# Roots and reciprocals of the norms, taken token by token on a few columns in a two-block transformer kernel

## The chip, the cores and the metric

The kernel runs on one core of a Trainium2 chip. The metric is device time in microseconds (us), the median of several executions. The engines are TensorE (PE; PEld is its weight load), VectorE (DVE), ScalarE (ACT), GpSimd (POOL) and SyncE (SP), which issues most DMAs.

## The reference

Everything is float32. The input is one sequence of 256 tokens of width 1024, with 256 context and 256 memory tokens. The first block has two layers (latent attention, a Fourier mix and a convolution side by side, then an MLP); the second has one (RWKV-7, S5 and gated linear attention side by side, then cross attention, then a gated MLP). Between them stand the norms that this change is about. Each takes one number per token, or per token and head:

```python
def rms_norm(x, g):
    xf = x.astype(jnp.float32)
    y = xf * lax.rsqrt(jnp.mean(jnp.square(xf), axis=-1, keepdims=True) + EPS)
    return (y * g.astype(jnp.float32)).astype(x.dtype)
...
# in rwkv7_mix
kk = kk * lax.rsqrt(jnp.sum(kk * kk, axis=-1, keepdims=True) + 1e-12)
y = ((y - mean) * lax.rsqrt(var + RWKV_GN_EPS)).reshape(B, L, MIX_W) * ln_w + ln_b
# in gla_mix
o = o * lax.rsqrt(jnp.mean(o * o, axis=-1, keepdims=True) + 1e-5) * norm_g
```

## The kernel before

Activations lie with features on the 128 partitions and tokens on the free axis: `xT` and `hT` are 128 x 8 x 512 (8 feature tiles; 256 context tokens, then 256 tokens of x). Layer 0 of the first block works on all 512 tokens (`s` is 0:512), layer 1 and the second block on the last 256 (`xs`), except where keys of the context are needed.

**Order.** Each engine has its own instruction stream, written out by hand and in order. `did` (a helper) raises a semaphore behind an instruction, and mostly waits for it too. PSUM has 8 banks: `open_bank(key, pool)` in PE's stream takes the next one of a pool in turn and waits until its last user has freed it; `finished(engine, key)` waits until PE has filled it, `taken(engine, key)` until its reader has freed it. The pool "run" has banks 0 to 4 (and 7 in the second block), the pool "hold" has 5 and 6. The weights, most of the 247 MB read from HBM, come through `ring`, four slots of 1 MB, loaded by SP in the order of their use; PE frees a slot as it goes on to the next. A float32 matmul shows as two MATMUL and two LDWEIGHTS records in the trace, a transpose as one.

**A norm.** ACT squares the features into `sq` (L1257); for most norms POOL adds the first six or seven tiles (L1655). PE multiplies the squares by a 128x128 matrix of ones (`norm_stat_step`, `stat`), so that every partition of the bank holds the sum of each token. ACT takes the root of the bank, 128 x 256 or 128 x 512 elements, into `rinv` or `rinv2` (`root` L1262, `rooted` L1483). DVE takes the reciprocal of that in place (L1752, L1884, L1889, L1929, `recip` L2027) and multiplies the features by it (`scaled` L1754 and others). ACT then applies the modulation in the first block (`modulated`, `modulated_halves`, L1322), and PE goes on with a matmul on the result.

**The places**, in order of time:

- memory norm and the norm `("st", 0)` ahead of layer 0
- per layer: queries and keys (`stq`, `stkv`), the convolution's LayerNorm (`cvar`), the norm ahead of the MLP (`("st", 1)`, `("st", 3)`), the norm of the MLP's result (`("st", 2)` ahead of layer 1; `("st", 4)` ahead of the second block, with the final norm of the first block folded in)
- gated linear attention (`gos`, applied in `gla_end`), amid the loop over 16 S5 state tiles, in which DVE turns and scans `bu` n, POOL turns the states back, and PE fills its time with the tiles `rw`; each is copied to `raw` by ACT and shifted by DVE (`rw_tile`)
- RWKV: the key norm (`kks`), which is followed by gate tiles on PE, and the norm of the heads' outputs (`rv`), followed by the branch matmuls, of which `BRANCH_ORDER` puts six ahead of the first that reads `y_rw`
- the norms 6, 7 and 8. With 6 and 7 the next matmul runs on unscaled features, and the factor is applied to its result; 8 is the last norm.

Of the kernel before, what the change touches and what calls it, by code (L numbers as in the profile page):

```python
# [23 lines left out]
ALU = mybir.AluOpType  # L24
# [55 lines left out]
SUMMED = {0: 7, 1: 7, 2: 6, 3: 7, 4: 6, 6: 7, 7: 7, 8: 7}  # L80
SLOTS = 4
# [228 lines left out]
def two_blocks(nc, weights, vectors, table_in, x_in, ctx_in, mem_in, c_in, s5b_in, s5c_in, out):  # L310
# [3 lines left out]
    with ExitStack() as ctx:  # L314
# [21 lines left out]
        cs_raw = sb("cs_raw", [P, KD, 2])  # L336
        ps = ctx.enter_context(nc.psum_tensor("ps", [P, 8, 512], F32))
# [99 lines left out]
        def spage(i):  # L437
# [65 lines left out]
                  "pos_loaded", "square_sums", "h_half", "h_forms", "quad_sums", "first_product", "hid_forms", "x_next", "xmax", "xprob", "fconv", "fsilu", "fgate", "gains", "conv_first", "result")  # L503
# [60 lines left out]
        def _(pe):  # L564
# [80 lines left out]

            def norm_stat_step(key, norm, k, s, K=KD):

                n_sum = SUMMED[norm]
                if k < n_sum - 1:
                    return  # L650
                if k == n_sum - 1:
                    open_bank(key, "hold")
                    pe.wait_ge(S["square_sums"], SUM_ORDER.index(norm) + 1)
                    mm(bank(key)[:, s], ones, sq[:, 0, s], True, False)
                    return
                pe.wait_ge(S["squares"], KD * norm + (2 * k + 2 if norm == 4 else k + 1))
                mm(bank(key)[:, s], ones, sq[:, k, s], False, k == K - 1, key if k == K - 1 else None)
# [41 lines left out]
            for l in range(LAYERS):  # L699
                s = side(l)  # L700

                for i, n in enumerate(Z_ORDER):
# [16 lines left out]
                    if n == 4:  # L719

                        pe.wait_ge(S["lora_squares"], 3 * l + 3)
                        o_ = open_bank(("stq", l), "hold")
                        for k in range(2):
                            mm(o_[:, s], ones, sq[:, k, s], k == 0, k == 1, ("stq", l) if k == 1 else None)
                        o_ = open_bank(("stkv", l), "hold")
                        mm(o_[:, :], ones, sq[:, 2, :], True, True, ("stkv", l))
# [9 lines left out]

                pe.wait_ge(S["cq_ready"], 2 * l + 2)
# [91 lines left out]
                stat(("cvar", l), 2, lambda k: ctmp[:, k, s], lambda k: pe.wait_ge(S["conv_centred"], 2 * l + k + 1),  # L829
                     n=s.stop - s.start, c0=s.start)  # L830
                for n in range(1, WO_EARLY):
                    wo_early(n)
                for n in range(2):
# [7 lines left out]
                for n in range(KD + 2):  # L841
# [60 lines left out]
                for n in range(SUMMED[2 * l + 2] - 1, KD):  # L902
                    stat_of_x(n)

# [125 lines left out]
            for i in range(RW_FIRST):  # L1030
                rw_tile(i)
            for hh in range(2):
                taken(pe, ("go", hh))
                key = ("gos", hh)
                o_ = open_bank(key, "hold")
                mm(o_[:, :], ones, g_osq[:, 2 * hh:2 * hh + 2, :].rearrange("p a t -> p (a t)"), True, True, key)
# [24 lines left out]

            def head_sums(name, src, ready=None):
# [10 lines left out]
            head_sums("kks", r_b)  # L1073
            gate_tiles(3)
# [133 lines left out]
            for n in range(KD):  # L1208
                plain("xq", 0, n, ("xq", n), ready=(lambda k: pe.wait_ge(S["h2_ready"], KD + k + 1)) if n == 0 else None)
            pe.wait_ge(S["mem_back"], 16)  # L1210
# [31 lines left out]
            for m in range(2 * FT2):  # L1242
                plain("up", 0, m, ("up", m), ready=(lambda k: pe.wait_ge(S["h2_ready"], 2 * KD + k + 1)) if m == 0 else None)
            with_squares("down", "down", FT2, lambda k: fhid[:, k, :], lambda k: pe.wait_ge(S["fgate"], k + 1), 8)


        @block.scalar
        def _(act):
# [10 lines left out]
            def root(key, dst, s, scale, eps="eps6", name="root"):  # L1259

                finished(act, key)
                did(f(dst[:, s], bank(key)[:, s], ACT.Sqrt, bias=table(eps), scale=scale), key=key)  # L1262

# [1153 lines left out]
```

## Time and profile before

| | |
|---|---|
| median of 3 runs | 1874.79 us (1873.02 to 1876.01) |
| the profiled execution | 1872.94 us, span 1871.1 us |
| PE busy | 1764.5 us (94% of the span) |
| DVE busy | 925.8 us (49%) |
| ACT busy, POOL busy | 398.6 us (21%), 298.0 us (16%) |
| chain that ended last | PE 78%, DVE 13%, ACT 2%, DMA 2% |
| mean granted PE clock | 0.982 |

The span is the time from the first to the last instruction in the trace; the execution's own time has 1.84 us more. The chain that ended last is followed back from the last instruction, at each step to what released it.

### The profile page before, as it was taken

How to read it: one execution, taken by the hardware profiler on the slowest of the kernel's cores; microseconds unless marked ns; L12 is line 12 of the kernel's file. 1: busy time of each engine (PE TensorE's matmuls, PEld its weight loads, DVE VectorE, ACT ScalarE, POOL GpSimd, SP SyncE). 2: the span in 40 equal slices, each digit the busy share in tenths (PEclk: the TensorE clock that was granted, in tenths of full speed). 3: DMA queues.
4: the chain of work that ended last, by engine and by line, in shares of the span. 5: the costliest groups of instructions: out<-in, count | busy, mean ns of one | idle time of the engine just before them, and what ended most of it. 6: DMA issues, size and time to landing. Idle time of an engine off the chain costs nothing.

```text
span 1871.1 us, 25901 instructions
## 1 busy us (share of the span) xinstructions
PE 1764.5 (94%) x10456; PEld 1391.1 (74%) x10456; DVE 925.8 (49%) x1738; ACT 398.6 (21%) x757; POOL 298.0 (16%) x305
## 2 busy tenths in 40 slices
PE   7999999899999999899899999977999899999997
PEld 5434444488888888656899987855798688888886
DVE  1247542464676434575687643299621432255511
ACT  1312444221112210346221002210421101200000
POOL 0100252122001211005243110166000000000000
PEclk9999999999999999999999999888999999999999
DMA  7774483122333222321354554222312344244443
GB/s 291 308 288 185 161 323 127 67 71 88 113 135 113 81 79 88 112 68 52 130 179 159 177 180 138 91 95 108 113 48 92 113 158 135 91 158 153 144 154 112
DMA packets 38704, 256.22 MB, mean 137 GB/s; under 512 B 4128, under 2 KB 7328, under 8 KB 9024
## 3 DMA queue, kind: packets, MB, share of 16 engines
q1 hardware_dynamic: 36240, 240.86, 36.9%
q0 software_dynamic: 1776, 9.57, 1.3%
q10 hardware_dynamic: 576, 4.19, 0.5%
q8 instruction: 83, 1.36, 0.3%
q14 instruction: 29, 0.24, 0.0%
HBM read 247.27 MB, written 7.34 MB: 136 GB/s over the span
## 4 chain that ended last, share of the span: by engine, by line
PE 78%; DVE 13%; ACT 2%; DMA 2%; issue 2%; POOL 2%; SPq 0%; ACTq 0%; DVEq 0%; POOLq 0%
PE ps L595 77%; DMA ring<-weights 1%; DVE arena L1869 1%; PE ps L790 1%; DVE arena L2027 1%; DMA xT<-x_t 1%; DVE arena L2067 1%; DVE spare L2140 1%; DVE arena L2066 1%; POOL aux L1672 0%; DVE aux L1899 0%; DVE arena L1900 0%; DVE arena L1901 0%; ACT hT L1322 0%; POOL aux L1655 0%
## 5 line engine op out<-in xcount | busy, mean ns | idle before, releaser
L595 PE MATMUL ps<-hT,ring 128*128 128x256 f32 (+3 forms) x3184 | 739.6, 390 | 22.7 <-issue 17.0
L595 PEld LDWEIGHTS ps<-hT,ring 128*128 128x128 f32 (+1 forms) x3184 | 571.3, 193 | 181.3 <-issue 111.2
L595 PE MATMUL ps<-arena,ring 128*128 128x256 f32 (+3 forms) x1884 | 380.2, 358 | 5.0 <-DVE arena L1901 3.2
L595 PEld LDWEIGHTS ps<-arena,ring 128*128 128x128 f32 (+1 forms) x1884 | 317.6, 190 | 58.7 <-issue 13.3
L1655 POOL TENSOR_TENSOR aux<-aux 128x256 f32<-128x256 f32 (+1 forms) x46 | 50.0, 1088 | 611.0 <-ACT aux L1257 543.0
L595 PE MATMUL ps<-arena,sums 128*128 128x256 f32 (+1 forms) x768 | 136.5, 327 | 1.3 <-DVE aux L1965 1.3
L595 PEld LDWEIGHTS ps<-arena,sums 128*128 128x128 f32 x768 | 118.2, 191 | 12.3 <-DVE aux L1965 2.5
L1257 ACT ACTIVATE aux<-xT 128x256 f32<-128x256 f32 (+1 forms) x64 | 31.0, 494 | 285.7 <-DVE xT L2057 93.3
L1672 POOL TENSOR_SCALAR aux<-aux,small 128x512 f32<-128x512 f32 (+1 forms) x48 | 70.8, 1483 | 117.8 <-DVE small L1917 117.7
L1691 POOL TENSOR_TENSOR arena<-arena 128x256 f32<-128x256 f32 (+1 forms) x32 | 27.0, 843 | 332.4 <-ACT arena L1442 332.4
L595 PE MATMUL ps<-hT,sums 128*128 128x128 f32 (+1 forms) x512 | 78.6, 301 | 0.7 <-DVE aux L1965 0.4
L1869 DVE SCALAR_TENSOR_TENSOR arena<-arena,vec 128x512 f32<-128x512 f32 (+1 forms) x120 | 73.6, 614 | 3.2
L595 PEld LDWEIGHTS ps<-hT,sums 128*128 128x128 f32 x512 | 69.6, 191 | 4.7 <-DVE aux L1965 0.8
L1441 ACT ACTIVATE arena<-arena 128x1024 f32<-128x1024 f32 (+1 forms) x32 | 27.0, 844 | 209.8 <-DVE arena L1973 209.8
L1941 DVE TENSOR_TENSOR sums<-ring 128x512 f32<-128x512 f32 x64 | 44.1, 690 | 55.6 <-PE ps L595 54.5
L595 PE MATMUL ps<-arena 64*64 64x64 f32 (+3 forms) x1392 | 65.5, 234 | 2.5 <-issue 1.7
L595 PEld LDWEIGHTS ps<-arena 64*64 64x64 f32 (+2 forms) x1392 | 59.5, 143 | 8.8 <-issue 7.3
L1967 DVE TENSOR_TENSOR aux<-aux,ps 128x256 f32<-128x256 f32 x24 | 10.1, 421 | 105.7 <-PE ps L595 105.5
L1910 DVE TENSOR_REDUCE small<-ps 128x1 f32<-128x512 f32 (+1 forms) x48 | 28.9, 602 | 66.7 <-PE ps L595 66.1
L595 PE MATMUL ps<-spare,ring 128*128 128x256 f32 x256 | 60.6, 379 | 1.3 <-DVE spare L2007 1.3
L595 PE MATMUL ps<-spare,sums 128*128 128x256 f32 x256 | 57.9, 379 | 0.0
L1943 DVE TENSOR_TENSOR sums<-ring 128x512 f32<-128x512 f32 x64 | 54.6, 854 | 2.2
(334 smaller groups left out, 1831.8 us busy)
## 6 DMA issues: line engine op xcount, KB each, us to landing
ring<-weights SPq DMA_DIRECT2D x224, 1024.0 KB, 4.9
kept_turns<-aux ACTq DMA_DIRECT2D x4, 1024.0 KB, 5.7
arena<-kept_turns POOLq DMA_DIRECT2D x6, 512.0 KB, 4.6
kept_keys_values<-spare POOLq DMA_DIRECT2D x1, 2048.0 KB, 8.2
arena<-kept_keys_values POOLq DMA_DIRECT2D x1, 2048.0 KB, 8.1
tab<-tables SPq DMA_DIRECT2D x1, 1344.0 KB, 13.7
arena<-mem_t SPq DMA_DIRECT2D x2, 512.0 KB, 5.7
xT<-ctx_t SPq DMA_DIRECT2D x1, 1024.0 KB, 9.2
```

What stands on the lines that cost most here:

```text
L595: ins = nc.tensor.matmul(o_, lhsT, rhs, start=start, stop=stop, skip_group_check=True)
L790: ins = nc.tensor.transpose(o_[:, kt * P:(kt + 1) * P], prob[:, t % 4, kt * P:(kt + 1) * P], table("ident"))
L1257: did(f(sq[:, k, s], xT[:, k, s], ACT.Square), "squares", wait=False)
L1441: did(f(two, two, ACT.Relu))
L1655: did(nc.gpsimd.tensor_tensor(sq[:, 0, s], sq[:, 0, s], sq[:, k, s], ALU.add), "square_sums" if k == SUMMED[norm] - 1 else None)
L1672: did(nc.gpsimd.tensor_scalar(prob[:, t % 4, 0:nk], prob[:, t % 4, 0:nk], small[:, 3, t:t + 1], None, ALU.mult), "prob_ready", wait=False)
L1691: did(nc.gpsimd.tensor_tensor(t1, b12, b11, ALU.subtract))
L1869: did(v.scalar_tensor_tensor(dst, src, w, dst, ALU.mult, ALU.add), name)
L1910: did(v.reduce_max(small[:, 2, j:j + 1], bank(("s", l, j))[:, 0:nk], AX))
L1941: did(tt(s3, a11, a21, ALU.subtract))
L1943: did(tt(s2, a21, a11, ALU.subtract))
L2027: did(v.reciprocal(a, a))
```

## The change

Of all norms but the memory norm and `("st", 0)`, the sum over the features is now taken with the squares as the stationary operand and one column of ones as the moving one (`token_sums`; for the norms by head, `head_tokens` with the two columns of `headones` that stand for the heads). The result has tokens on the partitions and one column per tile of 128 tokens (for heads, two per tile). ACT takes the root of these 2 to 16 columns (`token_root`), DVE their reciprocal (`inverse`), into the small tile `roots`. A further matmul per 128 tokens spreads them back: the stationary operand is the column repeated 128 (or 64) times, the moving one the identity (`spread`, `head_spread`). DVE multiplies by the bank that this fills, in place of `rinv`.

```diff
+            def token_sums(key, src, tiles, first, last, a=0):
+                for t in tiles:
+                    mm(bank(key)[:, a + t:a + t + 1], src[:, t * P:(t + 1) * P], ones[:, 0:1], first and t == tiles[0], last,
+                       key if last and t == tiles[-1] else None)
+
+            def spread(key, name, tiles, c0=12, pool="hold"):
+
+                o_ = open_bank(key, pool)
+                pe.wait_ge(S["inverse"], INVERSES.index(name) + 1)
+                for t in tiles:
+                    mm(o_[:, t * P:(t + 1) * P], roots[:, 1, c0 + t:c0 + t + 1].to_broadcast([P, P]), table("ident"), True, True,
+                       key if t == tiles[-1] else None)
...
@@ PE, layer: behind the ab matmuls, behind wo_early(1), behind the wo tiles, behind the MLP
+                spread(("qb", l), f"q{l}", token_tiles_of(s), 0)
+                spread(("kvb", l), f"kv{l}", range(4), 4)
                 pe.wait_ge(S["cq_ready"], 2 * l + 2)
...
                 for n in range(1, WO_EARLY):
                     wo_early(n)
+                    if n == 1:
+                        spread(("cvb", l), f"conv{l}", token_tiles_of(s), 8)
...
+                spread(("nb", 2 * l + 1), 2 * l + 1, token_tiles_of(s))
...
+                if l == 0:
+                    spread(("nb", 2), 2, (2, 3))
+                    spread(("nbc", 2), 2, (0, 1))
+                else:
+                    spread(("nb", 4), 4, range(4))
...
@@ PE, second block
-                mm(o_[:, :], ones, g_osq[:, 2 * hh:2 * hh + 2, :].rearrange("p a t -> p (a t)"), True, True, key)
+                for i in range(2):
+                    for tt in range(2):
+                        c = 4 * hh + 2 * i + tt
+                        mm(bank(("gos",))[:, c:c + 1], g_osq[:, 2 * hh + i, tt * P:(tt + 1) * P], ones[:, 0:1], c == 0, True,
+                           ("gos",) if c == 7 else None)
...
                 s5_filler(2 * m)
+                if m == 1:
+                    for hh in range(2):
+                        spread(("glab", hh), "gla", range(4), 4 * hh, "run")
                 s5_out(m)
...
+            def head_spread(name, inverse):
+
+                for half in range(2):
+                    key = (name, half)
+                    o_ = open_bank(key)
+                    if half == 0:
+                        pe.wait_ge(S["inverse"], INVERSES.index(inverse) + 1)
+                    for t in range(4):
+                        for hh in range(2):
+                            c = 2 * (4 * half + t) + hh
+                            mm(o_[64 * hh:64 * hh + 64, t * P:(t + 1) * P], roots[:, 1, c:c + 1].to_broadcast([P, 64]),
+                               table("ident"), True, True, key if t == 3 and hh else None)
...
-            head_sums("kks", r_b)
-            gate_tiles(3)
+            head_tokens(("kks",), r_b)
+            gate_tiles(1)
+            head_spread("kkb", "rw_k")
+            gate_tiles(2)
...
-            head_sums("rv", r_e)
+            head_tokens(("rv",), r_e)
...
             for n, b in BRANCH_ORDER:
+                if (n, b) == BRANCH_ORDER[1]:
+                    head_spread("rvb", "rw_y")
...
@@ PE: spread(("nb", 6)) behind the first xq tile, ("nb", 7) behind the first up tile, ("nb", 8) at the end
@@ ACT
-            for hh in range(2):
-                rooted(("gos", hh), flat2(page(8), hh), 1.0 / GDV, "eps5")
+            token_root(("gos",), 0, 0, 8, 1.0 / GDV, "eps5")
...
@@ DVE
+            def inverse(a, b):
+                did(v.reciprocal(roots[:, 1, a:b], roots[:, 0, a:b]), "inverse")
...
                 taken(dve, ("stq", l))
-                did(v.reciprocal(rinv[:, s], rinv[:, s]))
+                inverse(2 * l, 4)
+                taken(dve, ("stkv", l))
+                inverse(4, 8)
+                finished(dve, ("qb", l))
...
@@ DVE, the loop over the S5 state tiles n
-                if n in (4, 8):
-                    gla_end(n // 4 - 1)
+                if n == 0:
+                    taken(dve, ("gos",))
+                    inverse(0, 8)
+                if n in (4, 5):
+                    gla_end(n - 4)
...
             for half in range(2):
-                finished(dve, ("kks", half))
+            taken(dve, ("kks",))
+            inverse(0, 16)
             for n in range(4):
                 did(v.tensor_tensor_scan(r_b[:, n, :], table("scan"), r_lw[:, n, :], 0.0, ALU.mult, ALU.add),
...
@@ DVE: with norms 6 and 7 the filled bank is copied to rinv
```

## Rows read from the trace of the kernel before

**Rows 1.** The page, busy time of each engine.
```profile
PE 1764.5 (94%) x10456; PEld 1391.1 (74%) x10456; DVE 925.8 (49%) x1738; ACT 398.6 (21%) x757; POOL 298.0 (16%) x305
```

**Rows 2.** Groups by form, DVE: reciprocals (busy us, mean ns, idle before).
```profile
L2027 DVE RECIPROCAL arena<-arena 128x512 f32<-128x512 f32 x6 | 20.1, 3353 | 7.9 <-ACT arena L1483 7.8
L2027 DVE RECIPROCAL rinv<-rinv 128x256 f32<-128x256 f32 x5 | 8.8, 1751 | 4.8 <-ACT rinv L1262 4.5 <-ACT rinv L1493 0.3
L1781 DVE RECIPROCAL small<-small 128x16 f32<-128x16 f32 x1 | 0.3, 253 | 0.0
```

**Rows 3.** Timeline, PE: short matmuls (start, us, ..., idle before); then PEld by form.
```profile
162.29 0.97 PE L595 MATMUL ps<-tab,aux 128*128 128x32 f32 x8
917.03 1.06 PE L595 MATMUL ps<-hT,sums 128*128 128x128 f32 x8
873.08 2.00 PE L595 MATMUL ps<-aux,arena 128*64 128x128 f32 x32
...
L595 PEld LDWEIGHTS ps<-tab,aux 128*128 128x128 f32 x72 | 12.1, 190 | 3.1 <-issue 1.9
```

**Rows 4.** Timeline: the norm `("st", 1)` ahead of layer 0's MLP.
```profile
359.71 0.69 ACT L1262 ACTIVATE rinv<-ps,tab 128x512 f32<-128x512 f32 x1 [1.22 <-PE ps L595]
360.43 3.35 DVE L1752 RECIPROCAL rinv<-rinv 128x512 f32<-128x512 f32 x1 [2.60 <-ACT rinv L1262]
...
365.33 6.26 PE L595 MATMUL ps<-hT,ring 128*128 128x256 f32 x16 [5.65 <-issue]
...
374.60 1.99 PE L595 MATMUL ps<-spare,ring 128*128 128x256 f32 x8 [1.28 <-DVE spare L2007]
```

**Rows 5.** Timeline: the norm `("st", 4)`; then the last norm's root.
```profile
1120.95 0.42 DVE L2035 TENSOR_SCALAR rinv<-ps 128x256 f32<-128x256 f32 x1 [2.53 <-PE ps L595]
...
1122.39 1.75 DVE L2027 RECIPROCAL rinv<-rinv 128x256 f32<-128x256 f32 x1 [0.35 <-ACT rinv L1493]
...
1124.76 11.54 PE L595 MATMUL ps<-hT,ring 128*16 128x256 f32 x44 [3.85 <-issue]
...
1860.39 0.47 ACT L1262 ACTIVATE rinv<-ps,tab 128x256 f32<-128x256 f32 x1 [0.79 <-PE ps L595]
```

**Rows 6.** Windows: PE busy (x) ... PEclk, DMA share, GB/s, behind `("st", 4)`.
```profile
1124.00:1128.00 4.00, 3.24 (x8) 1.14 (x9) 3.96 (x10) 0.00 (x0) 0.00 (x0) 0.61 0.30 57
```

**Rows 7.** Timeline: layer 0, first matmul and first rotation of the queries.
```profile
176.67 16.87 PE L595 MATMUL ps<-arena,ring 128*128 128x512 f32 x38
...
179.36 0.70 DVE L1899 TENSOR_TENSOR aux<-ps,tab 32x512 f32<-32x512 f32 x1 [1.98 <-ACT arena L1367]
```

**Rows 8.** Timeline: layer 1, the last ab matmuls and the first rotation.
```profile
811.92 2.26 PE L595 MATMUL ps<-tab,arena 128*128 128x256 f32 x8
...
818.57 0.43 DVE L1899 TENSOR_TENSOR aux<-ps,tab 32x256 f32<-32x256 f32 x1
```

**Rows 9.** Timeline: the S5 loop, n = 1 to n = 4.
```profile
1210.55 0.69 DVE L2132 TENSOR_TENSOR spare<-ps,arena 128x512 f32<-128x512 f32 x1
...
1212.27 1.88 PE L595 MATMUL ps<-arena,tab 128*128 128x512 f32 x4
1214.50 1.13 PE L595 MATMUL ps<-aux,spare 32*128 32x256 f32 x8 [0.35 <-issue]
...
1212.94 1.28 ACT L1483 ACT_TABLE_LOAD   x1
...
1236.02 3.35 DVE L2027 RECIPROCAL arena<-arena 128x512 f32<-128x512 f32 x1
```

**Rows 10.** Timeline: RWKV's products behind the key norm.
```profile
1344.11 1.22 DVE L2178 TENSOR_TENSOR arena<-arena 128x1024 f32<-128x1024 f32 x1
...
1349.56 5.34 PE L595 MATMUL ps<-arena 64*64 64x64 f32 x175
```

**Rows 11.** Timeline: RWKV's output norm and the branches behind it.
```profile
1477.22 6.74 DVE L2027 RECIPROCAL arena<-arena 128x512 f32<-128x512 f32 x2 [7.76 <-ACT arena L1483]
...
1490.14 8.81 PE L595 MATMUL ps<-hT,ring 128*128 128x256 f32 x32 [3.87 <-DVE arena L2265]
```

More of the change, by code:

```diff
@@ L653, in norm_stat_step @@
                     pe.wait_ge(S["square_sums"], SUM_ORDER.index(norm) + 1)
[L654 to L657, printed above, removed]
+                else:
+                    pe.wait_ge(S["squares"], KD * norm + (2 * k + 2 if norm == 4 else k + 1))
+                first, last, i = k == n_sum - 1, k == K - 1, 0 if k == n_sum - 1 else k
+                if norm:
+                    token_sums(key, sq[:, i, :], token_tiles_of(s), first, last)
+                else:
+                    mm(bank(key)[:, s], ones, sq[:, i, s], first, last, key if last else None)
             open_bank(("mst", 0), "hold")
@@ L1262, in root, with token_root @@
                 did(f(dst[:, s], bank(key)[:, s], ACT.Sqrt, bias=table(eps), scale=scale), key=key)
+            def token_root(key, c0, a, b, scale, eps="eps6"):
+                finished(act, key)
+                did(f(roots[:, 0, c0 + a:c0 + b], bank(key)[:, a:b], ACT.Sqrt, bias=table(eps), scale=scale), key=key)
             act.wait_ge(S["silu_c"], 1)
@@ L1492, in _ @@
             act.wait_ge(S["x1_square"], 1)
[L1493 to L1494 removed]
+            did(f(roots[:, 0, 12:14], roots[:, 0, 12:14], ACT.Sqrt, scale=1.0 / D), wait=False)
+            did(f(roots[:, 0, 14:16], bank(("st", 4))[:, 2:4], ACT.Sqrt, bias=eps6, scale=1.0 / D), "x1_root")
             def gla_inputs(a, b):
@@ L1835, in _ @@
                     wait=False)
-            scaled(0, slice(0, 2 * T), ("st", 0))
+            taken(dve, ("st", 0))
+            did(v.reciprocal(rinv[:, :], rinv[:, :]))
+            for k in range(KD):
+                did(v.tensor_tensor(hT[:, k, :], xT[:, k, :], rinv[:, :], ALU.mult), "scaled", wait=False)
             mods(0, 0, 0, 4 * MOD_FIRST)
@@ L2169, in _ @@
             for half in range(2):
-                taken(dve, ("kks", half))
-                recip(flat2(r_e, half))
-            did(tt(r_kk[:, :, :], r_kk[:, :, :], r_e[:, :, :], ALU.mult))
+                key = ("kkb", half)
+                finished(dve, key)
+                did(tt(flat2(r_kk, half), flat2(r_kk, half), bank(key), ALU.mult), key=key)
             did(tt(r_at[:, :, :], r_kk[:, :, :], r_a[:, :, :], ALU.mult))
@@ L2249, in _ @@
                 did(stt(flat2(r_y, half), bank(("rm", half)), -1.0 / RD, flat2(r_y, half), ALU.mult, ALU.add), key=("rm", half))
+            taken(dve, ("rv",))
+            inverse(0, 16)
             for half in range(2):
-                taken(dve, ("rv", half))
-                recip(flat2(r_b, half))
-            did(tt(r_y[:, :, :], r_y[:, :, :], r_b[:, :, :], ALU.mult))
+                key = ("rvb", half)
+                finished(dve, key)
+                did(tt(flat2(r_y, half), flat2(r_y, half), bank(key), ALU.mult), key=key)
             for n in range(4):
@@ L2270, in _ @@
             taken(dve, ("st", 6))
-            recip(rinv[:, xs])
+            inverse(14, 16)
+            finished(dve, ("nb", 6))
+            did(v.tensor_copy(rinv[:, xs], bank(("nb", 6))[:, xs]), key=("nb", 6))
             for n in range(KD):
@@ L2287, in _ @@
             taken(dve, ("st", 7))
-            recip(rinv[:, xs])
+            inverse(14, 16)
+            finished(dve, ("nb", 7))
+            did(v.tensor_copy(rinv[:, xs], bank(("nb", 7))[:, xs]), key=("nb", 7))
             did(v.memset(fu[:, :, 0:2], 0.0), "fconv")
```

129 lines of the change are left out of this document (77 added, 52 removed).

## The prediction, on record before the run

> **What bounds the kernel now.** I read the page first. PE is busy for 94% of the span and DVE for half of it [rows 1], so a cheaper DVE instruction is worth something only where PE waits for it, and a matmul more costs its full time wherever PE does not wait. The groups by form give the size of what goes: a reciprocal of 128x512 takes 3.35 us and one of 128x256 1.75, while 16 columns take 0.25 [rows 2]. The change replaces 11 of the first kind (six at L2027 and five in the first block) and 10 of the second, 36.9 + 17.5 = 54.4 us of DVE. I then read the timeline around each of these places and noted how long PE stood still there. The reader should see four kinds: PE waits for the whole chain (the norms 1 to 4, the last one), PE waits for part of it (RWKV's output norm), PE does not wait at all (the convolution, RWKV's key norm, norms 6 and 7), and DVE itself is the bound (the loops that rotate the queries, the S5 loop). Last I read the granted clock in windows, since it falls behind some of these waits.
>
> **Prices.** A float32 matmul is two records. Eight records with 32 moving columns take 0.97 us, with 128 columns 1.06; without the tail of the last (0.27) that is 0.10 and 0.11 us a record. 32 records with 64 stationary columns, two of them side by side, take 2.00 us [rows 3]. No row has one moving column. I take 0.107 a record, between the two, so 0.21 a token tile; bounds are 0.03 (what the 64x64 records of rows 10 take: 5.34/175) and 0.19, the duration of the weight load [rows 3]. Then the sums cost PE what they cost before: four token tiles 0.86 us against one 512-column matmul (two records of 0.43), two tiles 0.43 against one of 256, the heads 1.9 against two of 512 (1.88 [rows 9]). The spreads are new: 0.22 us a token tile, 0.9 us for four, 0.45 for two, 1.9 for the heads' sixteen half-width ones. That is 48 tiles and two sets by head, 10.6 + 3.8 = 14.4 us of PE. A root or reciprocal of a few columns I take at 0.2 us, near the 0.25 for 16 columns [rows 2]; with eleven such steps on the path, 0.25 would add 0.5 us and nothing at all would take 2.2 away. The products now read PSUM; DVE's product over a bank takes 0.69 us for 512 columns [rows 9], and a new operand in PSUM should cost 0 to 0.1 each; I take none. The memsets that free banks are 0.1 each.
>
> **Norms on the chain.** In norm 1 root and reciprocal take from 359.71 to 363.8 us [rows 4]. Afterwards: root 0.25, reciprocal 0.2, spread 0.9 with 0.2 of latency, and the sums end 0.2 sooner: 4.1 becomes 1.6, 2.5 us less. The matmuls at 365.33 run at half clock, yet the next product waits for DVE's forms of `hT`, behind ACT's 16 pieces (the wait of 1.28 us) [rows 4]; they come 2.5 sooner whatever the clock, so that is all. Norm 2 (256 columns go ahead of the rest): 0.69 + 1.75 becomes 1.1, 1.4 less. Norm 3: 0.47 + 1.75 becomes 0.9, 1.4 less. Norm 8, the tail, the same (0.47 at 1860.39 [rows 5]): 1.3 less. Norm 4: from 1120.95 to 1124.14 the two DVE steps, root and reciprocal take 3.2 us [rows 5]; afterwards 0.2 x 5 for the small steps, 0.1, and a spread of four tiles, 1.1: 2.3, so 0.9 less. Behind its wait of 3.85 us the clock was 0.61 of full in the next 4 us [rows 6], and 44 records took 11.54 us where at 2.4 GHz they would take 44 x 0.22 = 9.7. With PE idle 1.2 us, working 0.9 and idle 0.6 I expect no fall to 1.2 GHz: 1.4 more (three quarters of 1.8). The Trainium skill (TensorE: Matmul & The Clock Gate, Part 1) has a throttled default that activity releases; by that rule the shorter waits keep the clock too, and it would give this term whole.
>
> **Queries.** Here the spreads are put behind the ab matmuls, on which PE was busy until it began the queries at 176.67 without a wait [rows 7]; the reciprocals had long been done. In layer 0 the change therefore adds: spread 0.9 + 0.2, DVE's two products 1.5, and only then PE's queries, at 179.3. Behind PE's first query come ACT's copy and DVE's rotation, which began at 179.36, 2.7 us behind PE; it begins 2.6 later, and that loop is DVE's (three steps of 0.7 a head against PE's 1.7), so all of 2.6 is lost. Layer 1: the ab matmuls end at 814.2, the rotation began at 818.57 [rows 8] because DVE first had to finish the 3.35 us reciprocal for the keys. Afterwards: spread 0.6, products to 815.9, first query and its copy to 817.6: 1.0 less.
>
> **Where PE did not wait.** The convolution's spreads, 0.9 and 0.5; norms 6 and 7, 0.45 each; RWKV's keys, 1.9. For the last, DVE's 6.7 us less buy nothing: it finished what PE's products need (L2178) at 1345.3, 4.2 us before PE came to them [rows 10], held up by exponentials that ACT issues behind PE's gate tiles, which themselves come 1.9 later. Sum 4.2 us more.
>
> **RWKV's output norm.** Of 6.74 us of reciprocals [rows 11] nothing stays, but the root now starts when all of the sums are done (0.8 later, behind a table load of 1.28). DVE has the inverse at 1477.6; the spreads start behind the first branch tile at 1477.7 and end at 1479.6; the products and the six steps behind them to `y_rw` are done at 1484.7, where before they were done just ahead of PE's 1490.14. PE adds 1.9 of spreads, and the two banks that these take make it wait 0.3 for DVE at the fourth further branch; it starts the first tile on `y_rw` at 1488.6, not 1490.14: 1.5 less. The 32 records behind the 3.87 us wait took 8.81, not 7.0 [rows 11]; that wait goes, so four fifths of 1.8: 1.5 more.
>
> **The S5 loop** is DVE's from 1210.55 on [rows 9]. Two reciprocals leave it, 6.7 us. But the inverse is put at n = 0, ahead of n = 1. PE reaches the sums at 1212.27 and ends them at 1214.1; only then ACT loads its table (1.28), the root follows, and DVE goes on at 1215.8: a new wait of 5.3 us. Queued behind it is n = 1, whose bank PE needs for n = 2 (it came 0.35 us too late already at 1214.50 [rows 9]). So PE stands still from 1214.1 to 1219.6, likely falls to half clock, and brings the next `rw` tile late: I put another 1.7 us on DVE for it. With the inverse's 0.2, 5.3 + 1.7 + 0.2 - 6.7 = 0.5, less 0.2 for fewer waits at POOL's side: 0.3 more. The spreads there, 1.8, lie in PE's own waits. Ends: 1.4 less if the clock holds; 2.5 more if PE is late twice.
>
> **Sum**: -2.5 -1.4 -1.4 -1.3 -2.3 (norms 1, 2, 3, 8, 4) +2.6 -1.0 (queries) +4.2 -3.0 (RWKV's output norm) +0.3 = -5.8 us. The profiled execution took 1872.94 us and would take 1867.1; it lies 1.85 under the median, so the median goes to 1869.0. What can be told from no change here is 0.2%, 3.7 us.
>
> **Rivals.**
> *The small matmuls are dear* (slower). 104 one- or two-column matmuls and 48 spreads are 304 records. If a full-height weight load is not hidden under its neighbour, each takes 0.19 instead of 0.107: 25 us more, some 2 of it hidden, 1892. Break-even is 0.126 a record (5.8/304 more). Against it: the eight 32-column records take 0.97 us together, though their loads add up to 1.52 [rows 3]. The Trainium skill (same page, Part 3: Packing small matmuls) says that a weight load overlaps a running matmul only when the row group differs, and speaks for this rival; the trace does not agree. Chance 0.10, most of it for prices of 0.13 to 0.15 a record, 1876 to 1882.
> *Given back by placement*: PE late more than once in the S5 loop, no clock returned, the query loss somewhat larger: -5.8 + 2.2 + 2.9 + 0.7 = 0, 1875. For it: every spread stands at a fixed place in PE's order, and two places already lose. Chance 0.25.
> *The S5 stall is short*: DVE makes up for it later in the loop, where POOL's steps and its own slow each other, and the loop gains 5: with the clock returned at all places, 1863. Chance 0.15.
> *The forecast*: 1865.5 to 1872.5, chance 0.50.
>
> **Numbers.** 1869, range 1862 to 1877: it leaves out most of the first rival and the far end of the third. Faster by over 0.2% (below 1871.0): 0.80 of the forecast, all of the third, a little of the second: 0.58. Within 0.2%: 0.30. Slower: 0.12.
>
> **What would show it.** Norm 1: PE's wait of 5.65 us becomes about 3.2 with a spread in it. Queries of layer 0: PE idle around 1 us ahead of its first query, the first rotation near 2.6 us later against the ab matmuls. S5: DVE idle 5 us ahead of n = 1. RWKV's keys: DVE idle where its reciprocals were. Output norm: PE's wait under 1 us. A single-column record away from 0.11 us makes the prediction wrong everywhere at once; a DVE wait at n = 0 that is not there, or a stall after it twice as long, makes it wrong by its own size.

## The result, and the profile after

The kernel with the change takes 1879.49 us (1874.54 to 1883.85, 20 runs); the kernel before, run beside it, 1874.73 us (1871.57 to 1878.45, 20 runs). The ratio is 1.0024, 95% interval 1.0016 to 1.0032: slower by 4.5 us, where 5.8 us less were forecast. Run a second time, unchanged, it gave 1.0017 (1.0006 to 1.0027). The direction is clear of noise; the size is 3 to 5 us.

The profiled execution of the changed kernel is the fastest of its 20: 1874.54 us, span 1872.7 us, mean granted clock 0.978. Its page, busy time and the chain that ended last by engine:

```profile
PE 1786.8 (95%) x10760; PEld 1428.4 (76%) x10760; DVE 874.6 (47%) x1749; ACT 391.2 (21%) x754; POOL 299.5 (16%) x305
...
PE 82%; DVE 11%; ACT 2%; DMA 2%; issue 2%; POOL 1%; SPq 0%; ACTq 0%; DVEq 0%; POOLq 0%
```

DVE lost 51 us, near the 54 forecast; PE gained 22.3 [rows 1], where 14.4 of spreads were forecast. The groups by form show what the new matmuls cost (busy us, mean ns, idle before):

```profile
L597 PE MATMUL ps<-tab,aux 128*128 128x1 f32 x136 | 19.2, 263 | 8.5 <-ACT aux L1329 5.9 <-ACT aux L1525 2.6
L597 PE MATMUL ps<-tab,roots 128*128 128x128 f32 x96 | 16.3, 324 | 3.9 <-DVE roots L1824 3.9
...
L597 PE MATMUL ps<-tab,arena 128*128 128x2 f32 x32 | 5.4, 299 | 3.3 <-ACT arena L1680 1.9 <-ACT arena L1635 1.4
L597 PE MATMUL ps<-tab,arena 128*128 128x1 f32 x40 | 4.6, 244 | 0.0
L597 PE MATMUL ps<-tab,roots 128*64 128x128 f32 x64 | 4.2, 284 | 0.0
```

The 208 records with one or two columns took 29.2 us, 0.140 each, the 160 of the spreads 20.5, 0.128 each; the forecast had 0.107 for both. But these are means over two speeds. The timeline has spreads at both: for the convolution in layer 0, and for norm 1.

```profile
306.95 1.05 PE L597 MATMUL ps<-tab,roots 128*128 128x128 f32 x8
...
359.87 0.26 ACT L1339 ACTIVATE roots<-ps,tab 128x4 f32<-128x4 f32 x1 [1.14 <-PE ps L597]
360.16 0.18 DVE L1824 RECIPROCAL roots<-roots 128x4 f32<-128x4 f32 x1 [2.10 <-ACT roots L1339]
360.49 2.04 PE L597 MATMUL ps<-tab,roots 128*128 128x128 f32 x8 [0.66 <-DVE roots L1824]
...
364.14 4.60 PE L597 MATMUL ps<-hT,ring 128*128 128x256 f32 x10 [1.61 <-issue]
```

Eight records take 1.05 us in one place and 2.04 in the other. Root and reciprocal have become 0.26 and 0.18 us instead of 0.69 and 3.35, and PE's longest wait 1.61 instead of 5.65 [rows 4], as forecast. Yet the spread, which was put at 0.9 us, runs at half clock. Norm 4 shows it more strongly:

```profile
1118.10 3.57 PE L597 MATMUL ps<-tab,aux 128*128 128x1 f32 x16 [2.64 <-ACT aux L1525]
...
1122.55 0.18 DVE L1824 RECIPROCAL roots<-roots 128x4 f32<-128x4 f32 x1 [0.29 <-ACT roots L1571]
...
1122.87 2.05 PE L597 MATMUL ps<-tab,roots 128*128 128x128 f32 x8 [1.20 <-DVE roots L1824]
...
1125.61 2.70 PE L597 MATMUL ps<-hT,ring 128*16 128x256 f32 x7 [0.69 <-issue]
```

The window row of these 10 us (busy time of PE, PEld, DVE, ACT, POOL, then PEclk, DMA share, GB/s):

```profile
1118.00:1128.00 10.00, 8.01 (x31) 6.17 (x32) 3.70 (x13) 1.10 (x5) 0.00 (x0) 0.51 0.51 184
```

PE worked 8 of 10 us, and the granted clock was 0.51, the lower level, nearly throughout. The forecast had expected this stretch at the upper one.

At the queries of layer 0 the steps came as written down: spread behind the ab matmuls, DVE's two products, a PE wait of 0.80, and the first rotation at 183.58, 4.2 us later than in [rows 7], of which 1.3 had been lost earlier.

```profile
178.04 1.95 PE L597 MATMUL ps<-tab,roots 128*128 128x128 f32 x16
...
179.20 1.53 DVE L1974 SCALAR_TENSOR_TENSOR arena<-arena,vec,ps 128x512 f32<-128x512 f32 x2 [10.69 <-PE ps L597]
180.78 4.56 PE L597 MATMUL ps<-arena,ring 128*128 128x512 f32 x10 [0.80 <-DVE arena L1974]
...
183.58 0.69 DVE L1988 TENSOR_TENSOR aux<-ps,tab 32x512 f32<-32x512 f32 x1 [0.78 <-ACT arena L1444]
```

In the S5 loop DVE waits 4.09 us ahead of n = 1, and PE 4.62 behind that; eight records then take 2.07 us for the 1.13 of [rows 9]. ACT's table load did not wait for the sums, as the forecast had it: it ran from 1211.55 to 1212.83, while PE worked on them until 1212.73, so only root and reciprocal stand behind the last sum, and the wait is 1.2 us shorter than the 5.3 forecast.

```profile
1210.89 1.84 PE L597 MATMUL ps<-tab,arena 128*128 128x1 f32 x16
...
1211.55 1.28 ACT L1339 ACT_TABLE_LOAD   x1
...
1213.22 0.20 DVE L1824 RECIPROCAL roots<-roots 128x8 f32<-128x8 f32 x1 [4.09 <-ACT roots L1339]
...
1217.35 2.07 PE L597 MATMUL ps<-aux,spare 32*128 32x256 f32 x8 [4.62 <-issue]
```

Behind RWKV's keys and at its output norm PE is at half speed again. 16 records of a gate tile take 5.11 us, eight of a branch tile 3.76, and the head sums 3.19 instead of the 1.9 forecast:

```profile
1326.25 5.11 PE L597 MATMUL ps<-hT,ring 128*128 128x256 f32 x16
...
1475.49 3.19 PE L597 MATMUL ps<-tab,arena 128*128 128x2 f32 x16 [1.85 <-ACT arena L1680]
...
1478.54 3.76 PE L597 MATMUL ps<-hT,ring 128*128 128x256 f32 x8
1478.76 1.28 ACT L1339 ACT_TABLE_LOAD   x1 [3.52 <-PE ps L597]
...
1482.23 2.18 PE L597 MATMUL ps<-tab,roots 128*64 128x128 f32 x32
...
1490.05 1.99 PE L597 MATMUL ps<-hT,ring 128*128 128x256 f32 x8 [0.26 <-DVE arena L2362]
```

**Place by place.** Every kernel here runs the same weight matmuls in the same order, so the start of each can be set against its start in the trace before. The table gives what each stretch added (+) or saved, in us, one profiled execution per column. The names are those of the experiments below; *before 2* is the kernel before, profiled again. The row "ahead" holds also how much later than in the first profile the first weight matmul began, 0.3 to 1.4 us in the others. "norm 4" ends and "S5 loop" begins at 1200, amid a stretch at the lower clock.

```
                    before 2    after  a_again   b_wide   f_gla2   d_rest  c_chain   c_wide   g_best  h_three  i_q0old
ahead        0- 170    +0.9     +1.4     +2.5     +1.3     +3.1     +1.8     +0.3     +0.2     +0.8     +0.6     +1.6
queries 0  170- 190     0.0     +2.8     +2.9     +2.9     +2.8     +2.8      0.0      0.0     +1.2     +1.2      0.0
weights    190- 296    -3.6     -5.0     +2.8     -2.9     -6.3     -1.5     -3.2     -3.1     -4.4     -3.2     -4.0
conv 0     296- 340     0.0     +1.0     +1.0     +1.0     +1.0     +1.0      0.0      0.0      0.0     +1.0      0.0
norm 1     340- 502    +1.1     -1.4     -0.2     -2.2     -2.3      0.0     -0.2     -2.2     -2.2     +0.3     -1.3
norm 2     502- 811    +2.1     +0.7     +2.4     -1.0     +0.7     +1.4     +0.7     -1.0     -1.0     +0.8     -1.0
queries 1  811- 850    -1.0     -0.8     -1.8     -1.8     -0.8     -0.6     -0.8     -2.0     -2.9     -2.7     -0.5
conv 1     850- 886     0.0     +0.7     +0.7     +0.7     +0.7     +0.7      0.0      0.0      0.0     +0.7      0.0
norm 3     886-1100    +1.1     -0.3     +0.4     +0.2     -0.3     +0.8     -0.1     -0.9     -0.6     +0.5      0.0
norm 4    1100-1200    +1.5     -1.3     +1.1     -3.0     -1.3     -1.3     -1.3     -4.5     +0.7     +1.4     +0.8
S5 loop   1200-1320    -0.1     -0.1     -1.9     -1.8     -4.3     +1.6     -0.1     -0.7     -6.3     -6.1     -6.3
keys      1320-1343     0.0     +3.8     +3.9     +3.9     +3.9     +2.2      0.0      0.0      0.0     +2.2      0.0
scan      1343-1472     0.0      0.0     +1.6     +0.1      0.0     +1.8     +1.6     +1.6     +1.8      0.0     +2.1
out norm  1472-1500    -0.1     +0.2     -1.5     -1.4     +0.2     -1.4      0.0      0.0     -2.7     -2.7     -2.7
6 and 7   1500-1700     0.0     +0.9     +0.9     +1.0     +0.9     +0.9      0.0      0.0      0.0     +0.9      0.0
tail      1700- end     0.0     -1.0     -1.0     -0.9     -1.0      0.0     -1.0     -0.9     -0.9     -0.9     -0.9
```

Two things are to be seen first. *before 2* differs from *before* by 1 to 2 us at each of the norms 1 to 4, with nothing changed: the profile that the forecast used was a lucky one there (its mean clock is 0.982, while the mean over 23 executions of this kernel is 0.979). And "weights", a stretch that the change does not touch, varies by 9 us; only medians decide a few microseconds, and the table gives a hint of where they are.

### The profile page after: what moved, and what is told of

It reads as the page before. It is cut to its first block, busy times and chain, and to the rows that moved or that the text cites. A ratio compares the mean times of both kernels' runs of the same rounds, so it can differ in the third digit from the quotient of the medians.

```text
span 1872.7 us, 26549 instructions
## 1 busy us (share of the span) xinstructions
PE 1786.8 (95%) x10760; PEld 1428.4 (76%) x10760; DVE 874.6 (47%) x1749; ACT 391.2 (21%) x754; POOL 299.5 (16%) x305
## 4 chain that ended last, share of the span: by engine, by line
PE 82%; DVE 11%; ACT 2%; DMA 2%; issue 2%; POOL 1%; SPq 0%; ACTq 0%; DVEq 0%; POOLq 0%
PE ps L597 81%; PE ps L813 1%; DMA ring<-weights 1%; DVE spare L2232 1%; DVE arena L2159 1%; DMA xT<-x_t 1%; DVE arena L2158 1%; POOL aux L1746 0%; DVE aux L1988 0%; DVE arena L1989 0%; DVE arena L1990 0%; ACT hT L1399 0%; DVE ps L2225 0%; DVE spare L2224 0%; POOL aux L1729 0%
```

## Experiments

In all of them the old form can be kept at chosen places (`NEW` lists the places in the new form), and the rest is the changed kernel. The edits are shown against the changed kernel, with the values that hold in each run written out.

**1. a_again: the changed kernel, unchanged.**

> The changed kernel once more, beside the others of this call. Its first profile was one of its fastest executions (1874.5 us against a median of 1879.5), so a second profile should show what the typical one has more. Clock theory: a small matmul of one or two moving columns leaves the clock free to fall, so the windows at 1.2 GHz lie elsewhere or are longer this time, 3 to 5 us in all, and a spread of four tiles takes about 2.0 us in them and 1.0 elsewhere. Rival (only more PE work, 14 us of spreads less what the waits give back): the same offsets at every place as in the first profile, and the spread of a few us comes from DMA waits. Time 1.002 to 1.003 of the kernel before.

1879.03 us (1875.58 to 1886.64, 11 runs), ratio 1.0017 (1.0006 to 1.0027). The slowdown repeats, at the small end. The profiled execution is the slowest of the eleven, 12.1 us above that of the first profile. Of these, 7.8 lie in the stretch "weights" and 5.3 at the norms 1, 2 and 4; the lower clock has 89 us instead of 83. So both theories have a part in the spread between executions, the stretch that streams weights the larger one.

**2. b_wide: the same sums, with 128 (or 64) moving columns.** All columns of a tile's (or a head's) result are the same, and ACT reads one of them.

```diff
-                    mm(bank(key)[:, a + t:a + t + 1], src[:, t * P:(t + 1) * P], ones[:, 0:1], ...
+                    mm(bank(key)[:, P * t:P * (t + 1)], src[:, t * P:(t + 1) * P], ones[:, 0:P], ...
...
-                did(f(roots[:, 0, c0 + a:c0 + b], bank(key)[:, a:b], ACT.Sqrt, bias=table(eps), scale=scale), key=key)
+                did(f(roots[:, 0, c0 + a:c0 + b], bank(key)[:, P * a:P * b:P], ACT.Sqrt, bias=table(eps), scale=scale), key=key)
```

> The sums are taken with 128 moving columns of ones (64 for gated linear attention, 64 of the head matrix for the heads) in place of 1 or 2; the same weight loads, the same result in each column, of which the root reads one. A record then costs 0.11 us instead of 0.10 to 0.11. Clock theory: the clock stays up over the sums, spreads of four tiles take 1.0 instead of 2.05 us, the half-clock windows at the norms 1 to 4, RWKV's keys and outputs go or shrink, and the kernel takes 4 to 8 us less than the changed one, about equal to the kernel before (1871 to 1875). Rival (the price is the number of matmuls and where they stand): no change against the changed kernel, 1879, or 1 us more.

1873.23 us (12 runs), ratio 0.9989 (0.9974 to 1.0003), on the same chip as a_again: 5.8 us faster (5.2 by the ratios), for matmuls with more columns. The intervals do not overlap. The mean granted clock is 0.979 to 0.988 in its twelve executions and 0.975 to 0.978 in the eleven of a_again, so these do not overlap either. The new matmuls by form:

```profile
L603 PE MATMUL ps<-tab,aux 128*128 128x128 f32 x136 | 20.0, 296 | 7.7 <-ACT aux L1373 5.2 <-ACT aux L1584 2.5
L603 PE MATMUL ps<-tab,roots 128*128 128x128 f32 x96 | 13.0, 279 | 3.9 <-DVE roots L1909 3.9
...
L603 PE MATMUL ps<-tab,arena 128*128 128x64 f32 x48 | 6.5, 295 | 3.3 <-ACT arena L1752 1.9 <-ACT arena L1703 1.4
...
L603 PE MATMUL ps<-tab,roots 128*64 128x128 f32 x64 | 3.9, 275 | 0.0
...
L603 PE MATMUL ps<-tab,arena 128*128 128x128 f32 x24 | 3.0, 275 | 0.0
```

The 208 wide records cost 29.5 us together, the narrow ones 29.2: the wider sums are free. The spreads, identical in both, fall from 20.5 to 16.9 us, and PE in all from 1786.8 to 1777.8. Norm 1, timeline, and below it the window row of its 8 us in this kernel and in the changed one:

```profile
360.75 1.16 PE L603 MATMUL ps<-tab,aux 128*128 128x128 f32 x8 [0.74 <-ACT aux L1373]
...
362.56 1.13 PE L603 MATMUL ps<-tab,roots 128*128 128x128 f32 x8 [0.66 <-DVE roots L1909]
```

```profile
360.00:368.00 8.00, 4.99 (x27) 1.00 0.12 19
```

```profile
359.80:368.00 8.20, 5.93 (x18) 0.50 0.19 46
```

With the wait ahead of the spread the same (0.66 us), the clock is 1.00 with wide sums and 0.50 with narrow ones.

The clock falls behind narrow sums even where PE did not wait at all. In layer 0 the 24 records of the queries' sums run right behind other matmuls and take 2.7 us in either form (from 163.82 to 166.50 in a_again, from 164.28 to 167.04 in b_wide). The 16 weight records that follow them, first in a_again and then in b_wide:

```profile
166.50 8.81 PE L603 MATMUL ps<-hT,ring 128*128 128x512 f32 x16
...
167.04 7.03 PE L603 MATMUL ps<-hT,ring 128*128 128x512 f32 x16
```

The window row from 167 to 172 us of a_again has PE busy throughout and a clock of 0.66:

```profile
167.00:172.00 5.00, 5.00 (x9) 2.11 (x8) 0.36 (x2) 0.63 (x3) 0.00 (x0) 0.66 0.00 0
```

Of the four kernels with narrow sums here, three (a_again, f_gla2, d_rest) have such a fall, and the first profile of the change has none; of the eight profiles with wide sums or the old form, none has one.

**3. c_chain and d_rest: one part of the change each.** c_chain has the new form at the norms 1, 2, 3, 4, 8 and the queries of layer 1, where PE waits; d_rest has it everywhere else.

```diff
-NEW = ALL_SITES
+NEW = (1, 2, 3, 4, 8, "q1")                                                # c_chain
+NEW = ("q0", "conv0", "conv1", "gla", "rw_k", "rw_y", 6, 7)                # d_rest
```

> The change at the norms 1, 2, 3, 4 and 8 and the queries of layer 1 alone, the old form everywhere else. Clock theory: the profile of the changed kernel has -1.4, +0.8, 0, +1.3, -1.0 and -1.0 us there, so -1.3 in all, 1873.5, no difference from before that can be measured. Rival (the chains gain as predicted, -7.9 with -1.0 for the queries, and all of the loss lies where PE does not wait): 1866.

> The other half: the change at the queries of layer 0, both convolutions, gated linear attention, RWKV's keys and outputs, and norms 6 and 7; the old form at the rest. By the offsets of the first profile: +2.8 (lost again in the waits for weights by 270 us), +1.4, -0.5, +3.1, +0.7, +0.9. Clock theory: 3 of it come from the two-column sums of RWKV, so +5 us, 1880. Rival (placement only): +4.2 and the S5 loop's stall, the same within 1 us; the two are told apart by b_wide, this run says how the loss divides.

c_chain: 1868.24 us (6 runs), ratio 0.9953 (0.9939 to 0.9967), 8.8 us less than before. d_rest: 1884.44 us (6 runs), ratio 1.0043 (1.0029 to 1.0058), 8.1 more. The 1873.5 expected of c_chain was wrong by 5 us, and too little of a gain; its rival, that the chains gain as predicted and the loss lies elsewhere, had 1866 and came closer. The forecast's own terms for these six places add up to -9.9, within the interval of c_chain (-6.2 to -11.4); those for the places of d_rest to +4.1, against +8.1 (+5.4 to +10.9). So the change is a gain and a loss of like size in one. The halves add up to -0.7 with some 4 us of uncertainty, and the whole is +3.2 to +4.5; whether the rest is an interaction or uncertainty is not settled. The clocks of all executions point to an interaction: by them the lower level has 77 us in c_chain and 78 in d_rest, as in the kernel before (77), and 86 in the whole change.

**4. before_again: the kernel before against itself.**

> The kernel before once more, for a second profile of it: the profile on which the prediction rests took 1872.9 us, under the median, and showed three waits ahead of norms (st 1, 3, 4) followed by 3.4 to 6.8 us at half clock. Clock theory: where the clock falls changes from execution to execution by one or two such stretches, and in the stretch between 200 and 290 us, where the weights come at some 330 GB/s, up to 4 us either way. Rival: the two profiles agree within 1 us at every place, and the offsets of the changed kernels against the first are the whole truth. Time 1.000.

1874.5 us, ratio 0.9995 (0.9986 to 1.0005). The time is the same, but the mean granted clock is 0.979 and not 0.982. A mean clock c means that 2 x (1 - c) of the span passed at the lower level: 67 us in the first profile, 77 in this one, 83 and 89 in the two of the changed kernel, 47 with wide sums. Single profiles are not typical here: by the mean over all executions it is 77 us before, 86 in the changed kernel (both times) and 61 in b_wide.

**5. f_gla2: the inverse for gated linear attention at n = 2.**

```diff
-                if n == 0:
+                if n == 2:
                     taken(dve, ("gos",))
                     inverse(0, 8)
```

> The changed kernel with one edit: DVE's wait for the root of gated linear attention, and the inverse, stand at n = 2 of the S5 loop, not at n = 0. Stall theory (the prediction's): the wait of some 5 us in front of n = 1 and PE's of 4.6 us go, and the loop ends 4 to 7 us earlier: 1873 to 1875. Rival (the loop is bound by POOL or by PE at half clock once the reciprocals are gone): under 2 us.

1872.95 us (1869.32 to 1876.21, 11 runs), ratio 0.9994 (0.9985 to 1.0002), 4 to 6 us below the changed kernel. The timeline has neither stall:

```profile
1212.41 1.13 PE L603 MATMUL ps<-aux,spare 32*128 32x256 f32 x8 [0.29 <-issue]
...
1220.78 0.20 DVE L1909 RECIPROCAL roots<-roots 128x8 f32<-128x8 f32 x1
```

PE's wait of 4.62 us is one of 0.29, and DVE takes the reciprocal without waiting. In the table the loop now gives -4.3, against -0.1 and -1.9 in the two profiles of the changed kernel (-1.8 in b_wide, +1.6 in d_rest) with the inverse at n = 0.

**6. c_wide: c_chain with wide sums.** The diffs of b_wide and c_chain together.

> The change at the norms 1, 2, 3, 4 and 8 and the queries of layer 1 alone, with 128 moving columns in the sums. Clock theory: the spreads run at full clock (1.0 instead of 2.0 us for four tiles) at norms 1, 2 and 4, so 3 us less than the same with one column: 1865. Rival (the wide sums helped in b_wide only at RWKV and in the queries): as with one column, 1868.

1862.21 us (6 runs), ratio 0.9942 (0.9923 to 0.996). By the ratios it gains 2 us on c_chain, and the intervals overlap, so the times do not settle it. The clocks do show a difference: over their six executions c_wide has 55 us at the lower level in the mean, c_chain 77 (in the two profiles 46 and 86). Norm 4 in c_wide, timeline and window:

```profile
1109.99 2.05 PE L603 MATMUL ps<-tab,aux 128*128 128x128 f32 x16 [2.53 <-ACT aux L1584]
...
1113.25 1.13 PE L603 MATMUL ps<-tab,roots 128*128 128x128 f32 x8 [1.21 <-DVE roots L1909]
```

```profile
1109.90:1119.00 9.10, 7.12 (x42) 4.65 (x43) 5.17 (x16) 1.32 (x6) 0.00 (x0) 1.00 0.72 262
```

The waits are those of the changed kernel (2.53 for 2.64, 1.21 for 1.20), and the clock stays at 1.00 where it was 0.51. Sixteen sums take 2.05 us instead of 3.57, eight spreads 1.13 instead of 2.05.

This is the best case and not the rule. In the four other profiles with wide sums the clock falls at norm 4 all the same, behind the same wait of 2.53 us. In g_best the sums take 3.40 us, and in h_three 10 us pass almost wholly at the lower level:

```profile
1109.79 3.40 PE L603 MATMUL ps<-tab,aux 128*128 128x128 f32 x16 [2.53 <-ACT aux L1584]
```

```profile
1118.00:1128.00 10.00, 7.93 (x31) 5.66 (x32) 4.03 (x14) 1.18 (x5) 0.00 (x0) 0.54 0.54 193
```

Around the norms 1 to 4 together (20 to 25 us around each), the profiles spent this much at the lower level: 31 to 34 us in the four with narrow sums, 14, 27 and 24 in the three with the old form (*before*, *before 2*, d_rest), and 10, 3, 10, 25 and 15 in the five with wide sums (b_wide, c_wide, g_best, h_three, i_q0old).

**7. g_best: what had won, together.** Wide sums, the inverse at n = 2, the old form for the convolutions, RWKV's keys and the norms 6 and 7, and the spreads for the queries ahead of the ab matmuls:

```diff
+                spread(("qb", l), f"q{l}", token_tiles_of(s), 0)
+                spread(("kvb", l), f"kv{l}", range(4), 4)
                 token_tiles = range(4) if l == 0 else range(2, 4)
                 for tt in token_tiles:
                     key = ("ab", l, tt)
...
-                spread(("qb", l), f"q{l}", token_tiles_of(s), 0)
-                spread(("kvb", l), f"kv{l}", range(4), 4)
                 pe.wait_ge(S["cq_ready"], 2 * l + 2)
```

> Put together from what has helped or should: wide sums; the change at the norms 1 to 4 and 8, at both queries with the spreads ahead of the ab matmuls, at gated linear attention with the inverse at n = 2, and at RWKV's output norm; the old form at the convolutions, RWKV's keys and norms 6 and 7. Against c_wide: queries of layer 0 0 to 1 us more, S5 loop 5 us less, output norm 2 to 3 us less. 1857 to 1861, or 0.991 of the kernel before. Rival (PE's added work eats it): 1866.

1860.01 us (6 runs), ratio 0.9922 (0.9908 to 0.9937): faster than both kernels. The queries of layer 0 now cost 1.2 us instead of 2.8. The output norm in its timeline:

```profile
1460.89 1.97 PE L603 MATMUL ps<-tab,arena 128*128 128x64 f32 x16 [1.85 <-ACT arena L1752]
...
1462.69 1.95 PE L603 MATMUL ps<-hT,ring 128*128 128x256 f32 x8
...
1465.01 1.97 PE L603 MATMUL ps<-tab,roots 128*64 128x128 f32 x32 [0.37 <-DVE roots L1909]
```

Behind the same wait of 1.85 us sums and branch tile take 3.8 us, where the changed kernel needs 6.8, and the stretch gives 2.7 us, near the 3.0 of the forecast.

**8. h_three: the whole change, with three edits.** Wide sums, the inverse at n = 2, early spreads for the queries; the new form at all places.

> The whole change at all its places, with three edits together: sums with 64 or 128 moving columns instead of one or two, the inverse for gated linear attention taken at n = 2 instead of n = 0, the spreads for the queries ahead of the ab matmuls. Theory (each of the three gives what it gave where it was tried: 5.8 us, 4.4 to 6 us, and 1.5 to 3 us, independently of one another): 1866, clearly faster than before, ratio 0.993 to 0.997. From the other side, the best version so far (1860.0) plus the places that it left in the old form (convolutions 1.4, norms 6 and 7 0.9, RWKV's keys 3.6 to 3.8): 1866. Rival (the gains overlap, since all of them come down to the clock that PE is granted behind a wait): 1870 or more. RWKV's key norm alone is expected to cost 3.7 us against the old form, 1.9 of spreads and some 1.7 because the gate tile between sums and spreads runs at a lower granted clock.

1864.11 us (5 runs), ratio 0.9938 (0.9924 to 0.9952). The three edits turn the change from 0.2% slower to 0.6% faster, 15 us, about the sum of what each gave. For the keys 3.7 us were expected and 2.2 came: here the clock did not fall behind the sums, and the gate tile took

```profile
1322.76 3.67 PE L603 MATMUL ps<-hT,ring 128*128 128x256 f32 x16
```

In b_wide it did fall there (+3.9), with the same wide sums, and in d_rest it did not (+2.2), with narrow ones: at this place one of two profiles with wide sums and three of four with narrow ones have the fall, which is too few to tell them apart.

**9. i_q0old: g_best with the old form in layer 0's queries.**

```diff
-NEW = ("q0", 1, 2, "q1", 3, 4, "gla", "rw_y", 8)
+NEW = (1, 2, "q1", 3, 4, "gla", "rw_y", 8)
```

> The best version so far with the queries of layer 0 back in the old form (sum over the features in one matmul of 512 columns, root and reciprocal of 128 x 512). Theory (in layer 0 the new form only adds PE work and a product from PSUM, since PE never waited there): 1.3 us less than the best version, 1858.7, ratio about 0.9915. Rival (the difference was the noise of one execution): no change from 1860.0, ratio 0.9922.

1857.55 us (1854.24 to 1863.96, 6 runs), ratio 0.9904 (0.9887 to 0.9922), the lowest of all, where 1858.7 was expected. Its interval overlaps that of g_best, so the times do not settle it; the table shows the 1.2 us gone.

## Why the prediction was wrong, step by step

The step that failed is one assumption in two places: that PE would work at the upper clock through the new small matmuls. It stands under *Prices* (0.107 us a record for sums and spreads) and under norm 4 ("With PE idle 1.2 us, working 0.9 and idle 0.6 I expect no fall to 1.2 GHz"). The forecast looked only at how long PE would be idle; the waits did become shorter, and yet the time at the lower level rose from 77 to 86 us in the mean of all executions. Widening the sums, which changes no wait and no order, brought it to 61 and gave 5.8 of the 10.3 us between forecast and result. So the record price was right at the upper clock (eight spreads in 1.05 us) and wrong at the lower (2.04), and for the whole change the clock term had the wrong sign. By the times, the miss does not lie where PE waits for the chain (c_chain: -8.8 against -9.9 forecast), but in the other half (d_rest: +8.1 against +4.1) and in what the whole loses beyond its halves, 4 to 5 us. The page TensorE: Matmul & The Clock Gate of the Trainium skill (Part 1) says that the gate follows how busy PE has lately been; here PE was busy 8.0 of 10 us at a clock of 0.51 in the changed kernel and 7.1 of 9.1 at 1.00 in c_wide, so busy time as the profile counts it does not tell the two apart, and the trace does not agree with the use that the forecast made of that rule. Between a_again and b_wide only the moving columns of the sums differ on PE; how the chip judges activity is not shown, nor why norm 4 fell to the lower level in four of the five kernels with wide sums.

Term by term, means of the profiles that have the place in the new form with narrow sums, against the mean of the two profiles of before (from the table); with wide sums each profile's value:

| term | forecast | measured | with wide sums |
|---|---|---|---|
| norms 1, 2, 3, 8 | -6.6 | -3.2 | -6.1, -7.1, -6.9, -1.5, -5.3 (mean -5.4) |
| norm 4 | -2.3 | -1.5 | -3.7, -5.2, -0.1, +0.6, +0.1 (mean -1.7) |
| queries 0 and 1 | +2.6, -1.0 | +2.8, -0.6 | with early spreads +1.2; -2.5, -2.2, 0.0 |
| convolutions, norms 6 and 7 | +2.3 | +2.6 | +2.6 |
| RWKV's keys | +1.9 | +3.4 | +3.9, +2.2 |
| output norm | -3.0 | -0.6 | -1.4 (b_wide), -2.6 (three) |
| S5 loop | +0.3 | -0.1 | -1.7 (b_wide); at n = 2: -4.2 to -6.3 |
| ahead of 170, and the scan | 0 | +1.4, +1.0 | +0.5, +1.1 |
| sum | -5.8 | +5.2 | |

The five values are those of b_wide, c_wide, g_best, h_three and i_q0old, in this order. The sum leaves out the stretch "weights".

- **Norms 1, 2, 3 and 8**: the mechanism was right. Behind narrow sums the four-tile spread took 2.04 us for 0.9 (norm 1), and in the profiles about half of the gain is lost; with wide sums most of it is back in four of five. By the times of c_chain less was lost than its profile says: that profile has the lowest mean clock of the six executions.
- **Norm 4**: -0.9 for the shorter path and -1.4 for a clock that would hold. It did not. With wide sums it held throughout only in c_wide, and the mean is no better than with narrow ones. The values vary by over 5 us, and the lower level also comes near the end of this stretch (from 1193 us in the first profile, from 1184 in c_wide).
- **Queries**: right. Layer 0 lost 2.8, and moving the spreads ahead gave 1.6 back, which is the part that was placement. The forecast took no account of what the narrow sums ahead of 170 us do to the clock (see below).
- **Keys**: the spreads are 1.97 us as forecast; 1.4 more is the gate tile, 5.11 us for the 3.67 that it takes at the upper clock.
- **Output norm**: the term needed a clock that holds. With it -2.6; with narrow sums +0.2, -1.4, +0.2 and -1.4 (the mean is the -0.6 of the table).
- **S5 loop**: the stall came where it was forecast, 1.2 and 0.9 us shorter (DVE 4.09 us and PE 4.62, for 5.3 and 5.5). One step of it was wrong: the 1.28 us of ACT's table load were not on the path, since the load ran while PE still worked on the sums. At the output norm, where the forecast had it on the path too, it is (from 1478.76, behind the last sum at 1478.68).
- **Ahead**: a place that the forecast left out. Behind the narrow sums of the queries the weight matmuls lose 1.2 to 1.8 us at the lower clock in a_again, f_gla2 and d_rest, without any wait of PE (experiment 2); the rest of this row is the start of the first weight matmul, which varies by 1.4 us.
- **Scan**: nothing of the change acts here. In six of the ten profiles of changed kernels, with narrow and with wide sums, a tile of weight matmuls falls to the lower clock (in c_wide the window from 1443 us has 0.57), in the two of before none. Why is open, and so is the interaction named under experiment 3.

Of the rivals, "given back by placement" had named the S5 stall and the queries, and their repair gave 4 to 6 and 1.6 us; but it ends at no change, and of the clock it holds only that none comes back. "The small matmuls are dear", with a chance of 0.10, reached the right side: the result lies in its 1876 to 1882, and its price of 0.13 to 0.15 a record is close to what the means show (0.128 and 0.140), with the wrong reason. Weight loads are not the cause, since wide sums have the same number of loads and the spreads behind them fell from 0.128 to 0.106 a record. Nor did the sum rest on a typical trace: the first profile of before had less loss at norms 1 to 4 than the second, 4.8 us with the queries of layer 1.

## What to carry to other kernels

A float32 matmul with one moving column saves next to nothing over one with 128 (24 records in 2.7 us in either form), and behind a run of them TensorE was more often found at its lower clock: widen it, since the extra columns cost nothing here. The widening makes the fall rarer over the whole kernel and does not exclude it. A cheaper instruction on another engine is worth its place only where TensorE waits for it; where it does not, every added matmul and every new wait counts in full, so the same edit gained 9 us at six places and lost 8 at the others. And a forecast that counts on the granted clock needs more than one profile of the kernel before.

## What the runs showed of the hardware

- With the same instructions in the same order, sums of 128 (or 64) columns in place of one or two raised the mean granted clock of the executions (0.975 to 0.978 in a_again, 0.979 to 0.988 in b_wide) and took 5.8 us off.
- The clock fell behind 24 one-column records although PE had not waited and was busy for all of the next 5 us (0.66 there in a_again).
- At norm 4, with PE's waits alike (2.53 to 2.64 us, then 1.20 to 1.21), the clock was 0.51 behind sums of one column (*after*), 1.00 behind sums of 128 in c_wide, and 0.54 behind sums of 128 in h_three: the columns shift how often it falls and do not decide it at one place.
- At the upper clock 16 sum records with 64 columns take 1.97 us, and 16 with 128 columns 2.05; at the lower, 16 with one column take 3.57.
- ACT's table load (1.28 us) can run while PE still works on what the root behind it reads (1211.55 us, S5 loop of the changed kernel), or begin only behind PE's last sum and stand on the path (1478.76, output norm).
- The same kernel's execution varies by 8 us in one stretch (190 to 296 us) that streams weights, far more than what most of the places here are worth.
